# Starting transfers and an operand split sooner, and routing 37 heads in 248 steps instead of 296

## The reference, cut to what matters

```python
x = x + merged @ w_out
h = rmsnorm(x, norm2)                       # (tokens, 1024)
q = (h @ w_q).reshape(B, 8, 2, 128)         # 8 heads, two halves
s1, s2 = q[:, :, 0] . keys1, q[:, :, 1] . keys2     # 128 scores each
v1, i1 = top_k(s1, 16); v2, i2 = top_k(s2, 16)
cand = v1[..., :, None] + v2[..., None, :]  # 256 candidates
top, pos = top_k(cand, 16)                  # 16 experts of 16384 a head
idx = i1[..] * 128 + i2[..] at pos;  g = softmax(top)
act = gelu(h . u[idx])                      # u, v: (16384, 1024)
x = x + sum(g * act * v[idx])
```

## Time and profile before

| | us |
|---|---|
| median of 3 runs (lowest, highest) | 3620.48 (3613.44, 3623.07) |
| profiled execution | 3617.48 |
| its span, first to last instruction | 3615.7 |
| PE busy | 3352.2 (93%) |
| DVE busy | 2882.7 (80%) |
| POOL busy | 2072.1 (57%) |
| ACT busy | 1525.4 (42%) |
| transfers | 1216.08 MB, mean 336 GB/s |

### The profile page before, as it was taken

The page is one execution under the profiler, slowest core; times in us unless marked ns, Lnnn a source line. Parts: engine busy times, 40 slices in busy tenths (PEclk is TensorE's granted clock), DMA queues, the critical chain, the costliest instruction groups (busy, mean ns, idle before and its releaser), DMA issues.

```text
span 3615.7 us, 46346 instructions
## 1 busy us (share of the span) xinstructions
PE 3352.2 (93%) x13366; PEld 2195.7 (61%) x13366; DVE 2882.7 (80%) x6788; ACT 1525.4 (42%) x3462; POOL 2072.1 (57%) x1831
## 2 busy tenths in 40 slices
PE   8999899989999997999799999999987799999988
PEld 7787655444443545676588888788854365655622
DVE  5499774167797876999998889889899898997765
ACT  5225576122442322233355555555543354544432
POOL 6322134056555654777766666667665666666675
PEclk9899999999999998999799999999988899999999
DMA  6415564698999998999999999999999999999999
GB/s 215 132 35 150 136 162 142 206 362 320 369 341 384 350 363 342 384 384 397 403 404 394 399 399 396 398 400 410 400 385 371 336 410 411 405 385 409 380 409 373
DMA packets 439081, 1216.08 MB, mean 336 GB/s; under 512 B 65234, under 2 KB 149366, under 8 KB 437935
## 3 DMA queue, kind: packets, MB, share of 16 engines
q0 software_dynamic: 239616, 872.52, 61.9%
q1 hardware_dynamic: 172922, 305.06, 24.4%
q10 hardware_dynamic: 26293, 35.54, 2.9%
HBM read 1124.84 MB, written 88.12 MB: 335 GB/s over the span
## 4 chain that ended last, share of the span: by engine, by line
PE 55%; DMA 12%; DVE 10%; issue 4%; ACT 1%; POOL 1%; ACTq 0%; SPq 0%; DVEq 0%; POOLq 0%
PE open_q_and_scores_ps L2828 18%; PE open_sums_ps L1937 8%; PE open_h_T_ps L1951 4%; PE open_rows_ps L2912 4%; PE open_q_and_scores_ps L2886 3%; DMA late_v_rows<-in_peer_v,late_kept_idx 3%; PE open_h_T_ps L2806 3%; PE open_sums_ps L2912 3%; DMA late_u_rows<-in_peer_v,late_kept_idx 3%; PE open_h_T_ps L2737 2%; PE open_q_and_scores_ps L2759 2%; PE open_h_T_ps L2812 2%; DVE late_x L3314 2%; DVE late_u_rows L3279 2%; DVE table_masked L3355 1%
## 5 line engine op out<-in xcount | busy, mean ns | idle before, releaser
L2686 POOL DMA_INDIRECT late_v_rows<-in_peer_v,late_kept_idx x573 | 551.0, 962 | 209.7 <-issue 135.1
L2673 POOL DMA_INDIRECT late_u_rows<-in_peer_u,late_kept_idx x320 | 467.4, 1461 | 261.8 <-DVE late_dots L3279 203.9
L3279 DVE CUSTOM_DVE_ANT_0 late_u_rows<-late_u_rows,open_rows_ps 128x1024 f32<-128x1024 f32 x432 | 521.5, 1207 | 10.6 <-DMA late_u_rows<-in_peer_u,late_expert_idx 10.0
L3314 DVE SCALAR_TENSOR_TENSOR late_x<-late_v_rows,late_weights,late_x 128x1024 f32<-128x1024 f32 x368 | 470.9, 1280 | 2.8 <-DMA late_v_rows<-in_peer_v,late_kept_idx 2.7
L2828 PE MATMUL open_q_and_scores_ps<-table_h_T_upper,table_u_T_upper 128*128 128x512 f32 x1024 | 423.4, 414 | 0.0
L2828 PE MATMUL open_q_and_scores_ps<-table_h_T_lower,table_u_T_upper 128*128 128x512 f32 x1024 | 401.7, 392 | 0.0
L2828 PE MATMUL open_q_and_scores_ps<-table_h_T_upper,table_u_T_lower 128*128 128x512 f32 x1024 | 401.3, 392 | 0.0
L2686 POOL DMA_INDIRECT late_u_rows<-in_peer_v,late_kept_idx x259 | 244.6, 944 | 124.6 <-issue 36.5
L1850 POOL DMA_INDIRECT open_u_rows<-in_peer_u,late_expert_idx x115 | 161.0, 1400 | 252.8 <-DVE late_dots L2284 127.6
L2912 PE MATMUL open_sums_ps<-late_v_rows,table_diag 128*128 128x512 f32 (+1 forms) x382 | 213.6, 678 | 46.4 <-DMA late_v_rows<-in_peer_v,table_twin_idx 17.1
L3029 ACT ACTIVATE table_u_T_lower<-open_h_T_ps 128x512 fp32r<-128x512 f32 x256 | 152.7, 596 | 213.5 <-PE open_h_T_ps L2812 213.5
(11 more groups left out here) (477 smaller groups left out, 7933.8 us busy)
## 6 DMA issues: line engine op xcount, KB each, us to landing
table_u_block<-in_peer_u SPq DMA_DIRECT2D x128, 512.0 KB, 7.8
scr_scores<-table_scores SPq DMA_DIRECT2D x32, 896.0 KB, 14.7
open_weight_columns<-in_w_in SPq DMA_DIRECT2D x64, 256.0 KB, 5.7
table_second_scores<-scr_scores SPq DMA_DIRECT2D x4, 4096.0 KB, 15.7
front_w_raw<-in_w_in SPq DMA_DIRECT2D x48, 256.0 KB, 5.1
table_first_scores<-scr_scores SPq DMA_DIRECT2D x3, 4096.0 KB, 16.3
scr_m<-open_gated SPq DMA_DIRECT2D x42, 256.0 KB, 6.0
late_v_rows<-in_peer_v,late_kept_idx POOLq DMA_INDIRECT x573, 10.1
```

The costliest lines, as they stand in the source:

```text
L2673: pool.indirect_dma_start(u[k % U_RING][:], None, io["peer_u"][0], bass.IndirectOffsetOnAxis(ap=rows_of(n), axis=0)).then_inc(s_u[k % U_RI ...
L2686: pool.indirect_dma_start(slot[:], None, io["peer_v"][0], bass.IndirectOffsetOnAxis(ap=rows_of(m), axis=0)).then_inc(arrived, 16)
L3279: dve.tensor_tensor_reduce(u[k % U_RING][:], u[k % U_RING][:], h2_rows, 1.0, 0.0, ALU.mult, ALU.add, dots[:, n % COLS:n % COLS + 1]).then_ ...
L3314: dve.scalar_tensor_tensor(rows[:], slot[:], weight_of(m), rows[:], ALU.mult, ALU.add).then_inc(s_vsum, 1)
```

## The change

- `ROUTE_SPANS`: heads 11 to 47 are routed in steps 144 to 392, 6.7 steps a head.
- w_q_high: pieces 4 to 7 are issued after the first half of the last unit of the opening, pieces 0 to 3 after the second (before: all after the second).
- w_q_low: its load moves from in front of SP's tile loop into iteration t = 0, behind the stores and loads of that iteration.
- h_T of the last tile is no longer stored and read back: ACT copies it from PSUM into `B.h` itself, ahead of h2_T. The three others are read back one iteration earlier (t = `NE - 2`).
- The blocks are loaded once 60 of 64 query heads are done.
- ACT makes `B.hh` in the front, at head 61 (`upper_h`), not at the start of the table; DVE makes `B.hl` at step 145, not 151.
- The stage buffers come first in their group of the memory plan. So that they are free before the first keys and one-hot rows are written over them, ACT waits in `keep_keys` for all stores of scores.

```diff
--- before.py
+++ after.py
@@ -1445,7 +1445,7 @@
 TABLE_UNITS, TABLE_STEPS = 2 * NK + 1, (150, 390)
 PICK_STEPS = {t: (398, 444) if t == FIRST_TABLED else (tile_start(t - 1) + 4, tile_start(t) - 2) for t in TABLED}
 LANE_ROUTES = 11
-ROUTE_SPANS = ((3, 28, 16, 16), (4, LANE_ROUTES, 28, 144), (LANE_ROUTES, NH * (FIRST_TABLED + 2), 144, 440)) + tuple(
+ROUTE_SPANS = ((3, 28, 16, 16), (4, LANE_ROUTES, 28, 144), (LANE_ROUTES, NH * (FIRST_TABLED + 2), 144, 392)) + tuple(
     (NH * t, NH * (t + 1), tile_start(t - 2) + 12, tile_start(t - 1) - 4) for t in TABLED[2:])
 
 
@@ -1482,8 +1482,8 @@
         self.buf = phase.sb(name, [P, self.pieces, source.shape[1]])
         self.ready = phase.sem(f"{name}_in_sbuf")
 
-    def load(self, sp):
-        for k in range(self.pieces):
+    def load(self, sp, some=None):
+        for k in some or range(self.pieces):
             sp.dma_start(self.buf[:, k, :], self.source[k * P:(k + 1) * P, :]).then_inc(self.ready, 16)
 
     def wait(self, eng):
@@ -1510,9 +1510,9 @@
         self.twin_idx, self.twin_g = sb("twin_idx", [P, NH, TOPK // 2], U32), sb("twin_gate", [P, NH, TOPK // 2])
         with Lent(nc, "right") as products:
             one = lambda name, shape, dt=F32: products.sb(f"table_{name}", shape, dt)
+            self.stage = [one(f"scores{b}", [P, HALF_TILES - 1, STAGE_BLOCKS, P // 2]) for b in range(2)]
             self.hl = one("h_T_lower", [P, KC, TABLE_COLS], F32R)
             self.u = [one(f"u_block{b}", [P, D]) for b in range(TABLE_RING)]
-            self.stage = [one(f"scores{b}", [P, HALF_TILES - 1, STAGE_BLOCKS, P // 2]) for b in range(2)]
             self.minus = one("minus_identity", [P, P], F32R)
         with Lent(nc, "right") as read:
             one = lambda name, shape, dt=F32: read.sb(f"table_{name}", shape, dt)
@@ -1788,11 +1788,14 @@
             if u == 2:
                 sp.wait_ge(s_done, S0 + 3)
                 load_conv(NT + 1)
+            if u + 1 == UNITS_OPEN:
+                sp.wait_ge(s_ulog, S0 + 2 * u + 1)
+                L.w_q[1].load(sp, range(KC // 2, KC))
             sp.wait_ge(s_ulog, S0 + 2 * u + 2)
             if u + 2 < UNITS_OPEN:
                 load_xT(u + 2)
             if u + 1 == UNITS_OPEN:
-                L.w_q[1].load(sp)
+                L.w_q[1].load(sp, range(0, KC // 2))
             if u == 2 * NT:
                 sp.dma_start(L.gain[:], io["norm2_w"][0].partition_broadcast(P)).then_inc(L.s_gain, 16)
                 sp.dma_start(L.x2[1][:], io["x_prompt"][0, P:2 * P, :]).then_inc(L.s_x[0], 16)
@@ -2558,7 +2561,7 @@
 
         def store_hT(t):
             sp.wait_ge(s_hT, S0 + t + 1)
-            if t in TABLED:
+            if t in TABLED[:-1]:
                 sp.dma_start(scr["hT"][t - FIRST_TABLED], h2T[:]).then_inc(s_hTout.sem, 16)
 
         def load_x2(t):
@@ -2614,8 +2617,6 @@
                 sp.dma_start(B.scores[h][:], scr["scores"][2 * k + h]).then_inc(s_sin[h].sem, 16)
 
         load_x_new(1)
-        sp.wait_ge(done.s_vsum, S0 + OPEN_STEPS)
-        L.w_q[0].load(sp)
         for t in range(NE + 1):
             if t < NE:
                 store_x2(t + 1)
@@ -2627,10 +2628,12 @@
             if t == 0:
                 load_x2(1)
                 load_h2(1)
-            if t == NE - 1:
+                sp.wait_ge(done.s_vsum, S0 + OPEN_STEPS)
+                L.w_q[0].load(sp)
+            if t == NE - 2:
                 sp.wait_ge(s_outp, S0 + NE + 1)
-                load_turned(range(len(TABLED)))
-        sp.wait_ge(s_q, S0 + HEADS)
+                load_turned(range(len(TABLED) - 1))
+        sp.wait_ge(s_q, S0 + HEADS - NH // 2)
         for b in range(NK):
             load_block(b)
             if b >= STAGE_BLOCKS and (b - STAGE_BLOCKS) % STAGE_BLOCKS == STAGE_BLOCKS - 1:
@@ -2955,6 +2958,9 @@
             act.wait_ge(s_q, S0 + NH * t)
             if t > FIRST_TABLED:
                 act.wait_ge(s_hTout.sem, s_hTout.start + 16 * (t - FIRST_TABLED))
+            if t == NE:
+                act.wait_ge(s_outp, S0 + NE + 1)
+                act.activation(B.h[:, :, (len(TABLED) - 1) * P:], chain_banks(t)[:].rearrange("p a (k t) -> p (a k) t", t=P), ACT.Copy)
             act.activation(h2T[:], chain_banks(t)[:].rearrange("p a (k t) -> p (a k) t", t=P), ACT.Copy).then_inc(s_hT, 1)
 
         def keep_query(R):
@@ -3010,11 +3016,19 @@
                     keep_turned(R)
                     if t < NE and R == NH * (t + 1) - 1:
                         keep_h2(t + 1)
+                    if R == HEADS - 3:
+                        upper_h()
                     yield
             store_side(HEADS - 2)
             keep_scores(HEADS - 1)
             store_side(HEADS - 1)
             yield
+
+        def upper_h():
+
+            act.wait_ge(s_hin.sem, s_hin.start + 16 * (len(TABLED) - 1))
+            act.wait_ge(s_hT, S0 + NE + 1)
+            act.activation(B.hh[:], B.h[:], ACT.Copy).then_inc(s_hh.sem, 1)
 
         def upper(b, half):
             act.wait_ge(s_uturn.sem, s_uturn.start + TURNS * b + half + 1)
@@ -3035,7 +3049,7 @@
                 act.wait_ge(s_sout[q % 2].sem, s_sout[q % 2].start + 16 * (q // 2))
             if b == 0:
                 act.wait_ge(s_sc, S0 + HEADS)
-                act.wait_ge(s_hTout.sem, s_hTout.start + 16 * len(TABLED))
+                act.wait_ge(s_hTout.sem, s_hTout.start + 16 * (len(TABLED) - 1))
             act.activation(L.first_kept[:, b, :], pQS[:, b % 2, 0:KEPT_TOKENS[0]], ACT.Copy)
             act.activation(B.kept[:, b, :], pQS[:, b % 2, KEPT_TOKENS[0]:SAM], ACT.Copy)
             act.activation(B.stage[q % 2][:, :, b % STAGE_BLOCKS, :], pQS[:, b % 2, SAM:TABLE_COLS].rearrange("p (a t) -> p a t", t=SAM), ACT.Copy).then_inc(s_stage.sem, 1)
@@ -3046,8 +3060,6 @@
             act.wait_ge(s_outp, S0 + NE + 1)
             act.activation(B.minus[:], c.ident[:], ACT.Copy, scale=-1.0).then_inc(s_const.sem, 1)
             act.activation(B.ident[:], c.ident[:], ACT.Copy).then_inc(s_const.sem, 1)
-            act.wait_ge(s_hin.sem, s_hin.start + 16 * len(TABLED))
-            act.activation(B.hh[:], B.h[:], ACT.Copy).then_inc(s_hh.sem, 1)
             for half in range(TURNS):
                 upper(0, half)
                 lower(0, half)
@@ -3066,6 +3078,9 @@
         def keep_keys(t):
             i = t - FIRST_TABLED
             act.wait_ge(s_spread.sem, s_spread.start + SPREADS * i + 1)
+            if i == 0:
+                for b in range(2):
+                    act.wait_ge(s_sout[b].sem, s_sout[b].start + 16 * (NK // STAGE_BLOCKS // 2))
             act.wait_ge(s_fpick.sem, s_fpick.start + PICKS * i)
             act.activation(B.first_keys[:], pH[:, 1, 0:P], ACT.Copy).then_inc(s_skept.sem, 1)
 
@@ -3381,7 +3396,7 @@
                 vector_sum(m)
             for _ in units_at(FRONT_UNITS, FRONT_STEPS, n - 2):
                 next(front_units)
-            if n == TABLE_STEPS[0] + 1:
+            if n == TABLE_STEPS[0] - 5:
                 lower_h()
             for R, piece in ROUTES_AT.get(n, ()):
                 route(R, piece)
```

## The result

The changed kernel takes 3596.22 us (3591.81 to 3600.79), the one before 3620.48: ratio 0.9939, 95% interval 0.9927 to 0.9951, or 22 us less (18 to 26). So it is faster, by well under the 39 us forecast, and inside the range.

What follows compares the result with a forecast made beforehand. It took PE to bound the table stage, DVE the stretches around it, transfers the tail. Terms of 16 + 8 + 15 = 39 us gave 3582 us (chance 0.48), range 3562 to 3606.

Steps and rivals of the forecast that it cites:

- Part 1: Query-weight loads (1302 to 1450): merged load 16 us sooner, w_q_low wait costs 2, w_q_high gives 2; 16 us gained.
- Part 2: Split of h and first blocks (1760 to 1788): first product 11 us sooner, less 3 for DVE's little lead; 8 us gained.
- My chain: Before the first table product: constants written by 1772.8, block turned 1.1 us, then 3.6 us, giving 1777.5, 11 us sooner.
- Part 3: Heads 11 to 47 routed in 248 steps, not 296: table stage unchanged, 15 us gained behind 2674.
- The limit by the transfers: Stretch 2674 to 2882: with DVE relieved, transfers are late next, so 14 to 25 us can go; 15 taken.
- the cover: Table stage: 44 us of DVE routing moved in front stay hidden under PE's matmuls; cost 0, from 0 to +55.
- Rival D: Table stage: DVE becomes the bound, its 3.1 us wait for exps per head being latency; 55 us more, 3637, chance 0.06.
- C: Rival: nothing to measure, early gains are given back in 1450 to 1760, DVE and transfers nearly full; 3620, chance 0.08.
- A: Rival: transfers, not waits, give the time, so only idle transfers put to work count; 30 us, 3590, chance 0.20.
- B: Rival: one term fails, w_q_low late takes 10 us or DVE short of rows; 3593 to 3606, say 3598, chance 0.18.
- The room that I had computed there: Table stage: transfers need 862 of 886 us at 410 GB/s, leaving 24 us of room, so earlier gains can be kept.
- 57 us: Upper ends of the three terms, 20 + 12 + 25; two thirds of it was taken for the range's lower end, 3562.

Runs made afterwards that it cites:

- exps_beside_gelu: Kernel before, routing untouched, with ACT's exps of heads 11 to 47 two steps sooner, right ahead of a gelu group: 3642.17 us, ratio 1.0068.
- weights_as_before: Changed kernel with both loads of the query weights back in their old places: 3606.01 us, ratio 0.9968 to the kernel before.
- lower_147: Changed kernel, but DVE writes the lower half of h at step 147, behind that step's dot, not at 145: 3592.65 us, ratio 0.9922.
- routes_as_before: Changed kernel without its routing edit, heads 11 to 47 routed up to step 440 again: 3608.04 us, ratio 0.9971 to the kernel before.
- routes_alone: Kernel before with only the routing edit, heads 11 to 47 routed up to step 392: 3606.77 us, ratio 0.9966.
- exps_apart: Changed kernel, with exps that would stand right ahead of a gelu group moved one step sooner: 3584.12 us, ratio 0.9906 to the kernel before.
- low_before_rows: Changed kernel, with w_q_low loaded ahead of the x2 and h2 row loads in iteration t = 0: 3593.4 us, ratio 0.9926.

## Why the prediction was right or wrong

**What bounds it.** PE in the table stage, DVE and then the transfers behind it, transfers in the tail: right. "From there to the end nothing changes" was right too, once the end of the stretch is dated by an event that the 4 MB load of scores can't cross: from the last sum of tile 3 to the end it is 733.0 to 735.8 us in ten of the eleven profiles, whichever routing they have, and 738.7 in the eleventh (exps_beside_gelu). Dated by the dot of step 447 the tail seems to get shorter, 747.7 to 751.5 us in the eight profiles with routes up to 392 against 754.5 to 757.1 in the three with 440, for the reason given with the result.

**Part 1, forecast 16 us, measured about 10** (ratio of weights_as_before against the changed kernel's). The mechanism was right in each step: store landed in 6 us, merged tile's wait gone. The term that was mis-sized is "So this wait may cost 0 to 3 us. I take 2": it costs 8.81 us. The other sign of this is the product behind the wait, 5.34 us for 3.62. My landing time of 1402 held (1398.5), but I compared it with PE coming at 1400, and PE came at 1389.7: besides the merged tile's 16 us, step 16 came 5 us sooner and PE's wait for w_q_high fell from 8.83 to 5.63 us. A wait that takes the place of another has to be dated on the new clock of its consumer.

**Part 2, forecast 8 us, measured 4 to 5.** The forecast took 3 of 11 us off for ACT's gelus that wait for DVE's dots. It was this, but larger. Waits in 1740 to 1770 of the changed kernel:

```profile
ACT late_gelu L3116 <- DVE late_dots L3294: 13.1, 1, 13.1
...
PE open_sums_ps L2768 <- ACT late_q L2969: 10.1, 1, 10.1
```

The 4.4 us of DVE at step 145 stand ahead of the dot of step 147, for which ACT's gelu waits, with the query heads behind it. In the kernel before, no wait of ACT for a dot from step 144 to the first product was longer than 2.7 us. With the split behind the dot (lower_147) 4.9 us of the loss came back. My chain listed what the product needs, not what ACT has ahead of it. Part of the rest comes from the new routing: with the routes as before (routes_as_before) the first product comes 28.6 us behind the dot of step 144, 7.8 us sooner than before the change, and ACT's wait is 8.6 us. Of the 3.1 us by which DVE comes sooner to the dot of step 147 there, 1.7 are a shorter wait for a value row, so how much the routing itself costs here stays open. The loads of h_T and of the first blocks were not run apart from the rest.

**Part 3, forecast 15 us, measured 12 (8 to 17, routes_alone), by two errors of opposite sign.** That the number came near is luck. Behind the table the gain was larger: from the last product to the last sum of tile 3, 207.8 to 187.5 us in these profiles and 207.8 to 187.7 in routes_alone against before, so 20 us and not 15. The limit by the transfers (14 to 25 us) was the right one. I took its lower end, and the stretch came to its middle. In front, "at 0 I take it for the table stage" was wrong: 11.6 us, in the ten blocks where PE waits. The stretches make this 9 to 10 us in sum and the medians 12; the profiled execution of routes_alone is 4.7 us above its median, so single profiles don't settle it closer. The step that failed is the cover. I checked that DVE's added 44 us fit under PE (they do, 833.20 of 898 us, 47 more than before), and I named as the risk that DVE would hold ACT. I did not look at where the new pace puts ACT's own instructions. Rival D had the place right (ACT's exps among the table's copies) and the cause and price wrong: no latency at each head, but two table loads in a row at 10 of 37 heads.

**Its slower rival and the others.** C (nothing measurable) and D are excluded by the interval. A gave 3590 and B 3598, and the time is between them. B came nearest: its 3593 to 3606 hold the time, and the sign that I had set for it, a wait of PE for w_q_low of over 5 us, is there with 8.81; it took some 6 us of part 1 and not 10, and B's other half, DVE short of rows, did not come. What B lacks is the loss in the table stage. The sign set for D was half met: a stage of over 890 us, but no gelu waiting for dots in it. A wait of over 5 us before the first keys did not appear; ACT wrote them 0.15 us behind the start of a gelu. A says that part 2 adds nothing and the table stage can't matter for the end; yet the 12 us by which that stage got shorter without PE's waits came out whole at the end (exps_apart), at 399 instead of 393 GB/s. The room that I had computed there was real.

**The range.** Its lower end is not what its words say: two thirds of 57 us below 3620 is 3582, the forecast itself, and 3562 is nearly the whole 57 us. The measured time is far from that end, so nothing hangs on it.

## What to carry to other kernels

Moving work in time changes the order in which an in-order engine meets it, even on engines whose amount of work does not change. After each such move, list for every engine in a bound stage what now stands next to what, and look first at pairs that cost more together than apart. Where two periodic streams share an engine, a pace that is a multiple of the other's keeps their phase (8 steps against 4 here), and another may visit every phase, the worst one too (6.7 against 4). And when a wait is removed, date the next one by the consumer's new time.

## What the runs showed of the hardware that I had not expected

A load of ACT's function table takes 1.283 us: the 50 loads ahead of the exps have a mean of 1283 ns, before and after, and the exps start 0.02 us behind one (1949.53 + 1.28 to 1950.83). One such load between two copies was hidden from PE. Two with exps and a gelu (3.1 us) cost it 0.7 us where they fell behind the last copy of a block and 1.7 us where they fell between the two halves (block periods 7.6 and 8.6 us against 6.9, five times each in the changed kernel; one more block of 8.6 us holds PE's wait for a block of u). The Trainium skill, ScalarE: Activation LUTs, What ACT_TABLE_LOAD costs, gives about 1283 ns for the load, and this trace agrees. It adds some 1380 ns of drain, 2.66 us for every switch; no row here shows that, since load, exps, load and gelu follow one another within 0.03 us, and the measurement decides.

The second: what an issue costs SP depends on its place in a burst. In the changed kernel SP issues twelve transfers of 512 KB in a row from 1361.71 on: merged tile, x, x2, h2 and the 8 pieces of w_q_low. The first ten take 0.32 to 1.17 us each, the last two 1.88 and 2.38. The first line below has those two. Where w_q_low goes ahead of the two row loads (low_before_rows), its 8 pieces are cheap, and the row loads, now eleventh and twelfth, are dear:

```profile
1368.57 4.31 SPq L1487 DMA_DIRECT2D late_w_q_low<-in_peer_w_q  x2
```

```profile
1361.74 5.23 SPq L1487 DMA_DIRECT2D late_w_q_low<-in_peer_w_q  x8
1367.08 3.31 SPq L2573 DMA_DIRECT2D late_x<-scr_x  x1
1370.81 1.98 SPq L2581 DMA_DIRECT2D late_u_rows<-scr_h  x1
```

In all seven profiles with such a burst the eleventh and twelfth take 1.7 to 3.3 us, and none in front of them more than 1.5. So a moved load can cost SP more than its old row says. The row of 8.61 us for w_q_high is not a case of this: it joins two groups of four with SP's wait for the second half of the unit between them, and the second group alone takes 1.75 us:

```profile
1301.62 1.75 SPq L1487 DMA_DIRECT2D late_w_q_high<-in_peer_w_q  x4
```
